# A fused two-layer decoder kernel: one layer's weight sums move to its gate_up, and the last down pass is taken tile by tile

## The reference, cut to what matters

```python
for l in range(DEPTH):
    ...
    h = rms_norm(x, norm_gains[l, 0]) * (1.0 + sc1) + sh1
    y = token_mixer(h, ...)
    x = x + g1 * rms_norm(y, norm_gains[l, 1])
    h = rms_norm(x, norm_gains[l, 2]) * (1.0 + sc2) + sh2
    y = (silu(gate) * up) @ w_down[l]      # gate, up = split(h @ w_gate_up[l])
    x = x + g2 * rms_norm(y, norm_gains[l, 3])
```

## Time and profile before

| | us |
|---|---|
| median of 3 runs | 2423.5 (2421.77 to 2423.53) |
| time of the profiled execution | 2426.57 |
| its span | 2424.8 |
| TensorE busy in it | 2340.6 (97%) |
| VectorE busy | 1633.5 (67%) |
| ScalarE busy | 979.3 (40%) |
| GpSimd busy | 212.9 (9%) |

### The profile page before, as it was taken

One profiled execution on the slowest core, in us unless ns is written; L12 is line 12 of the kernel. 1 busy time (PEld: TensorE's weight loads), 2 busy tenths in 40 slices (PEclk: granted clock), 3 DMA queues, 4 the chain that ended last, 5 costly groups with the idle time before them and its releaser, 6 DMA issues.

```text
span 2424.8 us, 30608 instructions
## 1 busy us (share of the span) xinstructions
PE 2340.6 (97%) x11394; PEld 1887.3 (78%) x11394; DVE 1633.5 (67%) x2762; ACT 979.3 (40%) x1870; POOL 212.9 (9%) x292
## 2 busy tenths in 40 slices
PE   7999899999999999999989989999999999999996
PEld 6787677788788888888778877777888888888884
DVE  6676677667877777576752667776686566655765
ACT  5321355544333333344753115555543333324453
POOL 0001100021000000220110100000200000003001
PEclk9999999999999999999999999999999999999998
DMA  7768501131455554662432471102323222318333
GB/s 284 253 218 245 161 19 36 35 114 69 152 181 172 170 195 139 180 207 97 130 113 65 165 247 62 27 27 79 113 70 96 79 79 82 97 48 263 126 109 133
DMA packets 210757, 311.30 MB, mean 128 GB/s; under 512 B 13063, under 2 KB 145080, under 8 KB 206640
## 3 DMA queue, kind: packets, MB, share of 16 engines
q1 hardware_dynamic: 186976, 227.52, 29.1%
q0 software_dynamic: 23632, 81.82, 10.4%
HBM read 243.48 MB, written 71.02 MB: 130 GB/s over the span
## 4 chain that ended last, share of the span: by engine, by line
PE 83%; DVE 7%; DMA 5%; issue 2%; ACT 2%; POOL 1%; SPq 0%; ACTq 0%; DVEq 0%
PE ps L2977 31%; PE ps L3016 15%; PE ps L2507 7%; PE ps L2509 7%; PE ps L2508 7%; PE ps L2857 6%; PE ps L2803 3%; DMA sums_d<-F 3%; PE ps L2834 3%; DMA F<-in_w_down 1%; PE ps L2822 1%; DVE ast L1864 1%; POOL st L876 1%; PE ps L2571 1%; DVE hT_plain L2097 1%
## 5 line engine op out<-in xcount | busy, mean ns | idle before, releaser
L2977 PE MATMUL ps<-hT,wsp 128*128 128x512 f32 x1440 | 333.5, 389 | 2.6 <-issue 2.6
L2977 PEld LDWEIGHTS ps<-hT,wsp 128*128 128x128 f32 x1440 | 270.0, 188 | 59.9 <-issue 4.0
L2507 PE MATMUL ps<-hT,wsp 128*128 128x512 f32 (+1 forms) x744 | 311.5, 419 | 0.0
L2509 PE MATMUL ps<-hT,wsp 128*128 128x512 f32 (+1 forms) x744 | 292.7, 393 | 0.0
L2508 PE MATMUL ps<-hT,wsp 128*128 128x512 f32 (+1 forms) x744 | 292.5, 393 | 0.0
L3016 PE MATMUL ps<-wsp,asp 128*128 128x512 f32 x1056 | 249.7, 392 | 0.2
L3016 PEld LDWEIGHTS ps<-wsp,asp 128*128 128x128 f32 x1056 | 198.1, 188 | 44.0 <-issue 1.0
L2977 PE MATMUL ps<-tsum,wasp 128*128 128x512 f32 x960 | 226.5, 392 | 0.1
L2977 PEld LDWEIGHTS ps<-tsum,wasp 128*128 128x128 f32 x960 | 180.1, 188 | 40.1 <-DVE wasp L2312 1.0
L2507 PEld LDWEIGHTS ps<-hT,wsp 128*128 128x128 f32 x744 | 142.6, 192 | 32.1 <-issue 8.6
L2509 PEld LDWEIGHTS ps<-hT,wsp 128*128 128x128 f32 x744 | 142.2, 191 | 31.3
(11 more groups left out here) (286 smaller groups left out, 4145.1 us busy)
## 6 DMA issues: line engine op xcount, KB each, us to landing
F<-in_w_mod SPq DMA_DIRECT2D x80, 512.0 KB, 5.1
raw<-in_w_in SPq DMA_DIRECT2D x48, 512.0 KB, 4.0
raw<-in_w_gate_up SPq DMA_DIRECT2D x48, 512.0 KB, 4.8
F<-in_w_down SPq DMA_DIRECT2D x22, 1024.0 KB, 5.8
sums_d<-F SPq DMA_DIRECT2D x22, 1024.0 KB, 8.1
raw<-sums_d SPq DMA_DIRECT2D x88, 256.0 KB, 3.1
F<-in_w_gate_up SPq DMA_DIRECT2D x40, 512.0 KB, 5.6
acts_d<-F POOLq DMA_DIRECT2D x38, 512.0 KB, 6.5
```

The source lines that it names most:

```text
L2507: mm(o, a(0), b(0), start=start, stop=False)
L2509: return mm(o, a(1), b(0), start=False, stop=stop)
L2977: last = mm(bank(j, p), block_of(p, z)[:, k * P:k * P + P], times(p, zz, k), start=p < B_A22 and k == 0 and z == 0 and zz == 0, stop=k == ...
```

## The change

It has three parts.

1. In layer 1 the sums of w_down are no longer formed in GLA, but in gate_up: the places are two others of F (`sums_late`), SyncE loads pair `k` at block k + 5 of its program, VectorE makes the four sums in three parts of block k + 4 (`late_sums`), where `mod_chunks` stands in layer 0, and SyncE stores it at its block k + 6. Layer 0 is as before. Waits of layer 1's GLA and heads for the stores are gone.
2. In layer 1 the last eleven steps (77 to 87, `alone`) multiply for tile 6 only; then 33 matmuls for tile 7 follow. The activations of these steps have places of their own in `acts_r`, no ring, and are made two to a step from step 73 on. VectorE's `add_out(2, 3)` and `y_mean(1, 7)` stand behind tile 6's `y_sum`.
3. The stores of the tiles 6 and 7 of layer 1 are started by SyncE, behind its last load of weights, and not by GpSimd.

```diff
@@ -276,8 +276,15 @@
-        def down_a(a, z):
+        def alone(l, a):
+            return l + 1 == L and a >= FINAL + KH
+        def down_a(l, a, z):
+            if alone(l, a):
+                c0 = HALF + HALF // 2 * z
+                return acts_r[:, a - FINAL - KH, c0:c0 + HALF // 2]
             r, c0, w = a % ARING, 0, HALF
@@ -288,17 +295,25 @@
-        def slot_last_used(a):
+        def slot_last_used(l, a):
+            if alone(l, a):
+                return min(a - 2 * ARING, FINAL + KH - 1)
             if a < FINAL:
-        def acts_at(s):
-            first = s + 2 if s + 2 <= FINAL else min(2 * s + 4 - FINAL, s + 4)
-            after = s + 3 if s + 3 <= FINAL else min(2 * s + 6 - FINAL, s + 5)
-            return range(first, min(after, ASTEPS))
+        def acts_from(l, s):
+            if s + 2 <= FINAL:
+                return s + 2
+            if l + 1 == L and s > FINAL + 6:
+                return min(2 * s - FINAL - 2, ASTEPS)
+            return min(2 * s + 4 - FINAL, s + 4, ASTEPS)
+        def acts_at(l, s):
+            return range(acts_from(l, s), acts_from(l, s + 1))
@@ -347,6 +362,9 @@
             return F[:, sums_at[z]:sums_at[z] + 4 * HALF]
+        def sums_late(z):
+            return F[:, 15360 + 4 * HALF * z:15360 + 4 * HALF * z + 4 * HALF]
@@ -544,11 +562,13 @@
             order = [q for t in range(NT) for q, z in sums_order(t)]
-            return l * 3 * KH + 3 * order.index(k)
+            return 3 * order.index(k) if l == 0 else 3 * (KH + k)
-            return 16 * (l * SUMS_A + k + 1) if k < SUMS_A else 16 * (l * SUMS_B + k - SUMS_A + 1)
+            if l == 0:
+                return 16 * (k + 1) if k < SUMS_A else 16 * (k - SUMS_A + 1)
+            return 16 * ((SUMS_A, SUMS_B)[k % 2] + k // 2 + 1)
@@ -750,17 +770,17 @@
-                def sums_load(k, z):
-                    sp.dma_start(sums_in(z).rearrange("p (a n) -> p a n", a=2),
+                def sums_load(k, z, into=sums_in):
+                    sp.dma_start(into(z).rearrange("p (a n) -> p a n", a=2),
                                  w_down.rearrange("l (a k p) n -> p l k a n", p=P, k=KH)[:, l, k]
-                def sums_store(k, z):
+                def sums_store(k, z, out=sums_in):
 ...
                     apart(sp)
-                    sp.dma_start(sums_d[l, k], sums_in(z)).then_inc(s_bs[z], 16)
+                    sp.dma_start(sums_d[l, k], out(z)).then_inc(s_bs[z], 16)
@@ -788,10 +808,9 @@
                     own_mods(ring_after(n))
-                sp.wait_ge(s_hl, nj(l - 1, 1, 7) + 1 if l else KT)
-                if l:
-                    sp.wait_ge(s_dp, l * ASTEPS)
-                sums_load(0, 0)
+                if l == 0:
+                    sp.wait_ge(s_hl, KT)
+                    sums_load(0, 0)
                 for f in range(16):
@@ -802,7 +821,7 @@
                     t = f - 3
-                    if t >= 0:
+                    if l == 0 and t >= 0:
                         for k, z in sums_order(t):
@@ -838,6 +857,16 @@
+                    if l and 5 <= j < 5 + KH:
+                        k = j - 5
+                        if k < 2:
+                            sp.wait_ge(s_tl, l * 16 + 16)
+                        else:
+                            sp.wait_ge(s_bs[k % 2], sums_moved(l, k - 2))
+                        sums_load(k, k % 2, sums_late)
+                    if l and 6 <= j < 6 + KH:
+                        sums_store(j - 6, j % 2, sums_late)
                     for q in mod_share(j - 1) if l + 1 < L else ():
@@ -846,7 +875,7 @@
                                      ).then_inc(s_ml[MRING + q % MRING], 16)
-                for z, k in ((0, SUMS_A - 1), (1, KH - 1)):
+                for z, k in ((0, SUMS_A - 1), (1, KH - 1)) if l == 0 else ((0, KH - 1), (1, KH - 2)):
                     sp.wait_ge(s_bs[z], sums_moved(l, k))
@@ -863,6 +892,11 @@
                     sp.dma_start(raw_down(w), src).then_inc(s_rd[w % WRING], 16)
+            outs = out.rearrange("(t p) d -> p t d", p=P)
+            for t in (6, 7):
+                sp.wait_ge(s_xs, yj(L - 1, 1, t) + 1)
+                sp.dma_start(outs[:, t, :], xt[t % 3]).then_inc(s_skew, 16)
+            sp.wait_ge(s_skew, 48)
@@ -1032,12 +1066,11 @@
                     x_root(l, 1, 6)
-                store(l, 1, 6)
-                if l + 1 < L:
+                    store(l, 1, 6)
                     x_root(l, 1, 7)
-                store(l, 1, 7)
+                    store(l, 1, 7)
                 for q in range(3):
-                    pool.wait_ge(s_st[q], uses_after(l, 1, q))
+                    pool.wait_ge(s_st[q], uses_after(l, 1, q) - (16 if l + 1 == L and q < 2 else 0))
@@ -1210,7 +1243,7 @@
                         act.wait_ge(s_mst, 16)
-                    if f == 7:
+                    if l == 0 and f == 7:
                         act.wait_ge(s_bs[1], sums_moved(l, KH - 1))
@@ -1440,8 +1473,8 @@
                     else:
-                        act.wait_ge(s_dp, steps_done(l, slot_last_used(a)))
-                    nc.scalar.activation(down_a(a, 0), acts_of(a), ACT.Copy).then_inc(s_ah, 1)
+                        act.wait_ge(s_dp, steps_done(l, slot_last_used(l, a)))
+                    nc.scalar.activation(down_a(l, a, 0), acts_of(a), ACT.Copy).then_inc(s_ah, 1)
 ...
@@ -1865,17 +1898,20 @@
-                def weight_sums(k, z):
+                def weight_sums(k, z, parts=range(3), at_z=sums_in):
                     at = sums_made(l, k)
-                    b11, b12, b21, b22 = [sums_in(z)[:, HALF * i:HALF * i + HALF] for i in range(4)]
-                    dve.wait_ge(s_bl[z], sums_moved(l, k))
-                    v.tensor_tensor(b22, b22, b12, ALU.subtract).then_inc(s_bt, 1)
-                    v.tensor_tensor(b12, b12, b11, ALU.subtract)
-                    dve.wait_ge(s_bt, at + 1)
-                    v.tensor_tensor(b11, b11, b22, ALU.add).then_inc(s_bt, 1)
-                    dve.wait_ge(s_bt, at + 2)
-                    v.tensor_tensor(b21, b21, b11, ALU.subtract).then_inc(s_bt, 1)
+                    b11, b12, b21, b22 = [at_z(z)[:, HALF * i:HALF * i + HALF] for i in range(4)]
+                    if 0 in parts:
+                        dve.wait_ge(s_bl[z], sums_moved(l, k))
+                        v.tensor_tensor(b22, b22, b12, ALU.subtract).then_inc(s_bt, 1)
+                        v.tensor_tensor(b12, b12, b11, ALU.subtract)
+                    if 1 in parts:
+                        dve.wait_ge(s_bt, at + 1)
+                        v.tensor_tensor(b11, b11, b22, ALU.add).then_inc(s_bt, 1)
+                    if 2 in parts:
+                        dve.wait_ge(s_bt, at + 2)
+                        v.tensor_tensor(b21, b21, b11, ALU.subtract).then_inc(s_bt, 1)
@@ -1886,7 +1922,7 @@
                                     ALU.mult).then_inc(s_gd, 1)
-                    for k, z in sums_order(t)[0:1]:
+                    for k, z in sums_order(t)[0:1] if l == 0 else ():
                         weight_sums(k, z)
 ...
@@ -1957,7 +1993,7 @@
                     else:
-                        if h == 2 and g == 0:
+                        if l == 0 and h == 2 and g == 0:
                             dve.wait_ge(s_bs[0], sums_moved(l, SUMS_A - 1))
 ...
@@ -2318,6 +2354,11 @@
+                def late_sums(j, part):
+                    if l and 4 <= j < 4 + KH:
+                        weight_sums(j - 4, j % 2, (part,), sums_late)
                 def mod_chunks(qs):
@@ -2373,6 +2414,7 @@
                     mod_chunks(share[0:1])
+                    late_sums(j, 0)
                     if j > PLAIN:
@@ -2386,11 +2428,13 @@
                     mod_chunks(share[1:2])
+                    late_sums(j, 1)
                     dve.wait_ge(s_sp, seven(l, j, B_A22))
 ...
                     mod_chunks(share[2:3])
+                    late_sums(j, 2)
                     if not more:
 ...
@@ -2488,9 +2532,10 @@
                     y_mean(1, 6)
-                    y_mean(1, 7)
                     y_mul(1, 6)
                     y_sum(1, 6)
+                    add_out(2, 3)
+                    y_mean(1, 7)
                     y_mul(1, 7)
@@ -3000,7 +3045,7 @@
                     pe.wait_ge(s_al, steps_done(l, s))
-                    for i in pairs_of(s):
+                    for i in pairs_of(s) if not alone(l, s) else ():
                         if k == 0:
@@ -3013,17 +3058,35 @@
                         for z, zz in ((0, 0), (0, 1), (1, 0)):
-                            last = mm(o, down_a(s, z)[:, c0:c0 + P], down_w(w, zz),
+                            last = mm(o, down_a(l, s, z)[:, c0:c0 + P], down_w(w, zz),
                                       start=(ph in (D_P1, D_P2, D_P7) and k == 0
 ...
                             last.then_inc(s_dq, 1)
-                    last.then_inc(s_dp, 1)
+                    if alone(l, s):
+                        if k == 0:
+                            pe.wait_ge(s_ca, added(l, 1, 2))
```

(24 more changed lines are left out.)

## The result

The changed kernel takes 2405.97 us (median of 4 runs, 2403.3 to 2410.5), the kernel before beside it 2422.64 us (4 runs, 2420.19 to 2423.53): a ratio of 0.9929, with a 95% interval of 0.9916 to 0.9941. It is faster by about 17 us.

The account below looks back on a forecast made before the run. TensorE was taken as the bound almost everywhere, except in layer 1's GLA and the program's end. Terms -11.45 + 0 + 1.1 - 1.0 = -11.35 us gave 2412.2 us from the median of 2423.5, range 2408 to 2416.5.

Parts of the forecast that it names:

- Sums out of GLA: Layer 1's GLA: without the sums, TensorE's gaps and the clock's dips go; gain 11.45 us, bounds 8.04 and 12.
- Sums into gate_up: Layer 1's gate_up: VectorE's added operations and the 1 MB transfers are covered; cost 0, bounds 0 and 1 us per block.
- Rival D: gate_up: VectorE waits for the 1 MB load block after block and TensorE for VectorE, so slower; chance 0.04.
- The tail: End of the last pass: TensorE's work is unchanged, VectorE's chain of four tiles ends the program, 1.1 us later.
- Rival A: End of the program: only one chain of 5.4 us follows the last matmul, so the tail gains; 2409.5 us, chance 0.17.
- The last two stores: Program's end: stores on SyncE's queue land and issue sooner than GpSimd's; gain 1.0 us, bounds 0.1 and 2.0.

Follow-up runs that it names:

- e9: Kernel before, without the stores and all but two loads of layer 1's sums, VectorE's 44 operations kept: 2409.89 us, ratio 0.9952.
- e2: Kernel before with only the last two stores (tiles 6 and 7) moved to SyncE: 2414.86 us, ratio 0.9976.
- e3: Kernel before with only the last eleven steps done for tile 6, then tile 7, stores still by GpSimd: 2423.88 us, ratio 1.0002.
- e5: Changed kernel, but GpSimd waits at its end until SyncE's two stores have landed: 2409.16 us, ratio 0.9945.
- e7: Changed kernel with additions of tiles 4 and 5 ahead of the last copies, tile 5's power ahead of tile 4's store: 2403.29 us, ratio 0.9916.
- e4: The whole changed kernel once more, on one chip with its parts: 2405.64 us, ratio 0.9931 to the kernel before.
- e6: Changed kernel without tile 7's power on GpSimd, tile 7 scaled by tile 6's: 2403.97 us, ratio 0.9916.
- e10: The kernel of e7 once more, on the same chip as e11: 2404.27 us, ratio 0.9916.
- e8: e7's kernel with tile 7's inverse root taken by ScalarE and VectorE instead of GpSimd: 2402.7 us, ratio 0.9922 to the kernel before.
- e11: The kernel of e8 once more, on the same chip as e10: 2404.63 us, ratio 0.9914.

## Why the prediction was wrong

*Sums out of GLA, -11.45*: right. Seven tiles take 105.2 us instead of 116.57, the gaps and the dips of the clock went together, and e9 shows the cause that the prediction read from the chain of waits. The clock's part that the prediction put to the second gap is there in the kernel before, and there is none behind the third:

```profile
1435.00:1440.00 5.00, 4.52 (x25) 3.64 (x26) 3.78 (x14) 2.51 (x6) 0.00 (x0) 0.66 0.84 252
1455.00:1460.00 5.00, 5.00 (x34) 4.13 (x35) 3.81 (x13) 3.04 (x6) 0.00 (x0) 1.00 0.52 214
```

So 8.04 + 2 x 1.7 = 11.4. The piece of the program that holds it shrank by 12.4 us; over the profiles this piece varies by 1 to 2 us where its code is the same (1557.4 to 1558.7 in before, e2 and e3, 1544.5 to 1546.4 with part 1).

*Sums into gate_up, 0*: right, to 0.02 us in 371. Rival D did not come: no wait of VectorE there names a load.

*The tail, +1.1*: right in its two terms, 2.01 us of idle time ahead of step 76 instead of 1.35 and 22.97 us behind it instead of 22.57 (2412.68 - 2390.11), and in its order. Of the sum it is +1.2 once the load in the piece is taken off. What the prediction did not ask is what the longer idle ahead of step 76 does to the clock; in the two profiles of the changed kernel it does nothing, in e3 and e5 it adds 0.3 to 0.5 us. Rival A, by which the tail gains, falls. e7 shows what A would have wanted: another order on VectorE and GpSimd, and its chain is 5.4 us behind the last matmul.

*The last two stores, -1.0*: **this step failed**, at the sentence "the span ends at 2424.8, about 8 us later, which I take as fixed". The price of the store itself was right in this profile, 2.6 us to land for 2.7 (e2 has 3.6). But the 8 us behind the landing were GpSimd's, whose program closed that late because it waited for its stores; with the stores on SyncE its last instruction is the power of tile 7, before the last product and sum, and its closing lies beside these and the store. The term is -6.9 (e2, alone: -7.6), not -1.0. By terms: -11.4 + 0 + 1.0 - 6.9 = -17.3 us, where 16.7 were measured and 11.35 forecast. A closing time that the trace shows once, behind one engine, does not say whether it belongs to the program or to that engine. The bound from below should have asked: what if it is GpSimd's? With the 6.9 measured since in place of 1.0, the forecast's sum is 2406.3.

The Trainium skill, DMA: Bandwidth & Descriptors, "Issuing engines are not separate DMA queues", says that starting DMAs from several engines at once saves only the time of initiating them. For the transfer itself this case does not settle it: SyncE's store lands after 2.6 us in the changed kernel and 3.6 in e2, GpSimd's after 3.7 before and 3.4 in e3. The 6.9 us are not in the transfer but in GpSimd's closing. By an estimate from the first-byte times in the same page's "Latency and other measured facts", 0.6 against 1 us, 0.4 of the 1.1 us between 2.6 and 3.7 would be explained; no run here shows it apart.

## What to carry to other kernels

Ask of the end of a program which engine closes last, and read the first engine's closing waits for it: an idle stretch behind the last landing can be one engine's own and move with its last instruction. In this kernel it paid to have GpSimd done some 8 us before the others, and to give the last stores to SyncE. A load that VectorE waited for in the middle of a chain cost 11.4 us here and the 44 operations on it nothing that shows: look for a place where the buffer is free a stage ahead before you move the operations. And a piece that holds a load is compared better with that load's time taken off.

## What the runs showed that was not expected

GpSimd's program ends 7.8 us behind its last instruction (after, e2, e4, e7: the same within 0.1 us) or 8.1 to 8.3 us behind the landing that it waits for last (before and e3, e5); SyncE's 0.4 us behind a landing (e6).

A 512 KB store from SyncE is waited for in two sizes, 2.3 us (after, e4, e5, e6, e7, e10) or 3.2 to 3.4 (e2, e8, e11), steady for a kernel. No cause was found.

Identical code before layer 0's block products took 629.5 to 636.6 us over thirteen profiles, more than the difference between most kernels here. Behind the x768 row, e7 and e10 repeat to 0.1 us and so do e8 and e11, where the medians of 4 to 6 runs scatter by 1 to 2; and where two profiles of one kernel differ there (after and e4), the chain names the load.

The longer idle of TensorE ahead of step 76, 2.0 us instead of 1.4, was followed by a fall of the clock in seven profiles of nine; none of the four with the short idle has one.
